# Both heads of an attention step in one instruction, projection groups in quarters on a bank of their own, bias tables asked for earlier, and x loaded tile by tile

## The reference, cut to what matters

```python
for l in range(DEPTH):                     # DEPTH = 4
    hp = modulate(rms_norm(xp, norm_g[l, 0]), sh1c, sc1c)
    if l % 2 == 0: yp = na_context(...); ys = na_latent(...)   # attention
    else:          yp = conv_module(...)                       # conv
    xp = xp + g1c * yp
    xp = xp + g2c * sq_relu_mlp(modulate(rms_norm(xp, ...)))
# attention, latent tokens: keys of an 8-row x 16-column neighbourhood
# with a relative bias, and 256 cached context keys without one
s_loc = einsum(q, k_block) * scale + bias;  s_ctx = einsum(q, k_ctx) * scale
p = softmax(concat([s_loc, s_ctx]));  o = p @ v
```

## Time and profile before

| | us |
|---|---|
| median of 3 runs | 2930.84 (2929.15 to 3099.0) |
| profiled execution, its own time | 2931.26 |
| its span, core 2, from first to last instruction | 2929.7 |
| spans of the eight cores | 2902.6 to 2929.7 |
| mean granted TensorE clock of core 2 | 0.930 |

### The profile page before, as it was taken

The page is one execution under the profiler, slowest core; times in us unless marked ns, Lnnn a source line. Parts: engine busy times, 40 slices in busy tenths (PEclk is TensorE's granted clock), DMA queues, the critical chain, the costliest instruction groups (busy, mean ns, idle before and its releaser), DMA issues.

```text
span 2929.7 us, 44923 instructions; the slowest of 8 cores (2902.6 to 2929.7 us)
## 1 busy us (share of the span) xinstructions
PE 2557.6 (87%) x15696; PEld 1130.2 (39%) x15696; DVE 1185.6 (40%) x1808; ACT 1068.7 (36%) x1887; POOL 208.6 (7%) x275
## 2 busy tenths in 40 slices
PE   1778778999998977999998788899999898789997
PEld 0323223444443532444443232234444354334443
DVE  0445444532324655423334444453232355642333
ACT  2435445520314345302233544563022424541123
POOL 1001010000000021000000010000000001200000
PEclk9879787999999988999999888899999998999998
DMA  9542233254542311444446222114553231113232
GB/s 196 115 80 37 41 55 66 43 102 89 110 90 44 66 28 33 77 96 94 94 73 124 41 41 41 34 30 87 97 105 72 44 75 33 30 29 58 44 58 87
DMA packets 107594, 202.24 MB, mean 69 GB/s; under 512 B 41904, under 2 KB 52144, under 8 KB 107376
## 3 DMA queue, kind: packets, MB, share of 16 engines
q0 software_dynamic: 76592, 154.23, 31.4%
q1 hardware_dynamic: 30784, 45.14, 4.7%
HBM read 315.02 MB, written 31.46 MB: 118 GB/s over the span
## 4 chain that ended last, share of the span: by engine, by line
PE 76%; DMA 7%; ACT 6%; issue 5%; DVE 5%; DVEq 0%; SPq 0%; ACTq 0%; POOL 0%; POOLq 0%
PE ps L639 44%; PE ps L1270 6%; PE ps L868 6%; DMA scr<-rpbp 3%; PE ps L661 3%; PE ps L825 3%; PE ps L1236 2%; PE ps L918 2%; PE ps L1394 2%; PE ps L963 2%; ACT hTs L617 2%; PE ps L567 1%; PE ps L921 1%; DMA xTs<-xT 1%; PE ps L977 1%
## 5 line engine op out<-in xcount | busy, mean ns | idle before, releaser
L639 PE MATMUL ps<-hTs,ring 128*128 128x512 bf16 x3072 | 687.5, 386 | 42.8 <-ACT hTs L617 41.8
L639 PE MATMUL ps<-big,ring 128*128 128x512 bf16 x3072 | 680.1, 379 | 0.4
L703 ACT ACTIVATE big<-ps 128x512 f32<-128x512 f32 x384 | 229.2, 597 | 801.1 <-PE ps L639 796.1
L639 PEld LDWEIGHTS ps<-hTs,ring 128*128 128x128 bf16 x3072 | 302.3, 99 | 416.1 <-issue 70.7
L705 DVE TENSOR_TENSOR big<-big 128x512 bf16<-128x512 f32 x384 | 266.0, 693 | 448.2 <-ACT big L703 448.2
L639 PEld LDWEIGHTS ps<-big,ring 128*128 128x128 bf16 x3072 | 299.4, 98 | 359.2
L677 DVE SCALAR_TENSOR_TENSOR xTs<-ps,mod,xTs 128x512 f32<-128x512 f32 x240 | 180.1, 751 | 551.1 <-PE ps L639 509.8
L560 ACT ACTIVATE scr<-xTs 128x512 bf16<-128x512 f32 x216 | 133.4, 626 | 409.4 <-DVE xTs L677 306.8
L936 ACT ACTIVATE scr<-scr 128x512 bf16<-128x512 f32 (+7 forms) x384 | 174.3, 500 | 258.8 <-DVE scr L988 125.5
L401 POOL DMA_DIRECT2D ring<-wall x140 | 100.1, 715 | 1896.9 <-PE ps L639 1003.8
L868 PE MATMUL ps<-hTs,ring 128*128 128x512 bf16 x768 | 226.2, 450 | 6.3 <-DVE scr L804 3.4
(11 more groups left out here) (90 smaller groups left out, 1916.5 us busy)
## 6 DMA issues: line engine op xcount, KB each, us to landing
ring<-wall POOLq DMA_DIRECT2D x140, 1024.0 KB, 9.8
vo<-big SPq DMA_DIRECT2D x48, 256.0 KB, 4.5
kTo<-big SPq DMA_DIRECT2D x48, 256.0 KB, 2.0
scr<-big SPq DMA_DIRECT2D x128, 54.0 KB, 3.1
xTs<-xT SPq DMA_DIRECT2D x3, 2048.0 KB, 25.3
yT<-scr SPq DMA_DIRECT2D x24, 256.0 KB, 2.2
scr<-rpbp POOLq DMA_DIRECT2D x32, 136.0 KB, 11.4
big<-ckT POOLq DMA_DIRECT2D x2, 512.0 KB, 7.3
```

Source lines behind the costliest of these rows:

```text
L639: ins = e.matmul(ps[pi][:, :], lhsT=w[:, kc, fc * fw:(fc + 1) * fw], rhs=src[:, kc, t * 512:(t + 1) * 512], start=(kc == 0), stop=(kc == n ...
L703: P.op("act", lambda e: e.activation(out=ta[:, :], in_=ps[pi][:, :], func=AF.Relu), reads=[ps_r[pi]], writes=[ta_r])
```

## The change

Five things change.

1. **Two heads, one instruction.** Banks 0 to 3 become two pairs of adjacent banks (`ps2`); step n uses pair n mod 2. The bias add and the exponential each treat both heads in one instruction of 128 x 2 x n. The add, exponential and table buffers are twice as long and half as many (2, 4, 2).
2. **Order and banks of the finish.** There are two output banks (5, 6) and one denominator bank (7). When the last step of a stretch has been multiplied, Ln is emitted, then the exponential of the step at hand, then Exp and the DVE multiply. The reciprocal lives in the conv taps' buffer `wr`, so the taps are now loaded at the start of each attention layer's MLP.
3. **Fills.** Projection groups are emitted as four parts of two matmuls, `build_T` stands behind each of the first four groups, and all of them, as well as the condition piece, use bank 4 (28 fills over 20 steps).
4. **Tables.** `hankel_load` for the pair after next stands at the end of a pair, ahead of `done_piece` and the condition piece; for pair 1 it stands before the first pair.
5. **x.** `xT` is stored tile by tile, in DRAM too, so that a tile is 16 KB in a row per partition, moved in rows of 8 KB in place of 2 KB. Tile 1 waits for weight piece 2 and tile 2 for piece 3. `norm_whole(1)` moves behind `ensure_h(0)` in front of value block 0, `norm_whole(2)` behind `ensure_h(1)` in front of block 4.

```diff
-    ps = [nc.alloc_psum_tensor(f"ps{i}", [128, 512], F32) for i in range(8)]
+    ps2 = [nc.alloc_psum_tensor(f"pp{i}", [128, 2, 512], F32) for i in range(2)]
+    ps = [ps2[i // 2][:, i % 2, :] for i in range(4)]
+    ps += [nc.alloc_psum_tensor(f"ps{i}", [128, 512], F32) for i in range(4, 8)]
...
-            out=xT[:, :, t * 512:(t + 1) * 512],
-            in_=xT_d.rearrange("(c p) t -> p c t", p=128)[:, :, t * 512:(t + 1) * 512]),
+            out=xT[:, t, :, :].rearrange("p c w -> p (c w)"), in_=xT_d[t], max_dma_last_dim=8192),
...
-            extra=[[], [(ring_sem[1], 16)], [(ring_sem[1], 32)]][t])
+            extra=[[], [(ring_sem[2], 16)], [(ring_sem[0], 32)]][t])
...
-        pi = next_ps(0, 4) if st.get("in_attn") else next_ps()
+        pi = 4 if st.get("in_attn") else next_ps()
...
+        if l % 2 == 0:
+            load_wr(l // 2)
...
-        NZ, NPT = 4, 8
+        NZ, NPT = 2, 4
+        rcp = wr[:, 0:1024].bitcast(F32)
...
-            pi = next_ps(0, 4)
+            pi = 4
...
-                if l == 0 and j == 0 and b == 4:
-                    late_x()
+                if l == 0 and j == 0 and b in (0, 4):
+                    ensure_h(b // 4)
+                    norm_whole(b // 4 + 1)
...
-            pi = next_ps(0, 4)
+            pi = next_ps() if pro else 4
...
+            if pro:
+                part(0, 8)
+                return []
+            return [lambda k0=k0: part(k0, k0 + 2) for k0 in range(0, 8, 2)]
...
-        OA = [4, 5]
-        SA = [6, 7]
+        hankel_load(2)
+        hankel_load(3)
+
+        OA, SA = [5, 6], 7
...
-                P.op("dve", lambda e: e.tensor_tensor(
-                    out=z[:, 0:n], in0=ps[b.pi][:, 0:n],
-                    in1=Tt[:, o0:o0 + k, :].rearrange("p o q -> p (o q)"), op=ALU.add),
-                    reads=[ps_r[b.pi], Tt_r], writes=[b.z_r])
+                P.op("dve", lambda e: e.tensor_tensor(
+                    out=z[:, :, 0:n], in0=ps2[pp][:, :, 0:n], in1=Tt[:, :, o0 * 64:o0 * 64 + n],
+                    op=ALU.add),
+                    reads=[ps_r[2 * pp], ps_r[2 * pp + 1], Tt_r], writes=[z_r])
...
+            P.op("act", lambda e: e.activation(out=pt[:, :, 0:n], in_=src[:, :, 0:n], func=AF.Exp),
+                 reads=src_r, writes=[pt_r])
...
+        def settle(n):
+            out = []
+            while len(pending) > n:
+                b, hp, o_i, last = pending.pop(0)
+                pv(b, hp, o_i)
+                if last is not None:
+                    finish_ln()
+                    out.append(lambda o_i=o_i, hp=hp, last=last: finish_mul(o_i, hp, last))
+            return out
...
-                hankel_load(2 * hp + 2)
-                hankel_load(2 * hp + 3)
...
+                for n in range(6):
+                    fills += qk_group(hp + 1, g[n][1], g[n][0], False)
+                    if n < 4:
+                        fills.append(lambda h=tb[n][0], hf=tb[n][1]: build_T(h, hf))
...
+                    pp = nstep % 2
+                    nstep += 1
                     q += 1
+                    scores(b, pp)
+                    if b.add is not None:
+                        b.add(pp)
                     while fills and (nf - len(fills) + 0.5) * nst <= q * nf:
                         fills.pop(0)()
-                    settle(LAG)
+                    pending.append((b, hp, o_i, tq if m == len(lst) - 1 else None))
+                    late = settle(LAG)
+                    exps(b, pp)
+                    for fn in late:
+                        fn()
...
+            if hp < 6:
+                hankel_load(2 * hp + 4)
+                hankel_load(2 * hp + 5)
             if hp % 2 == 0 and hp < 7:
                 done_piece()
...
-        if i == 0:
-            load_wr(1)
...
-    norm_whole(1)
```

More of the change, by code:

```diff
@@ new lines, in attn_layer, with ctx_step @@
+        class Step:
+            pass
+        def ctx_step(hp, qh, lc):
+            b = Step()
+            b.n, b.c0, b.first, b.v_r, b.add = 512, 0, lc == 0, cvb_r, None
+            b.ones = ones_c[:, :]
+            b.reads = [ckT_r, q_r[hp % 2][qh]]
+            b.lhs = lambda pb: ckT[pb:pb + 64, hp, lc * 128:(lc + 1) * 128]
+            b.rhs = lambda pb: qb[hp % 2][pb:pb + 64, qh * 512:(qh + 1) * 512]
+            b.gate = None
+            b.v = lambda h: cvb[:, lc, h * 64:(h + 1) * 64]
+            return b
@@ L959, in own_block, with own_step @@
+        def own_step(hp, qh, c, rows):
+            b = Step()
+            Tt, Tt_r = Tb[hp % 2]
             r0, k = rows[0], len(rows)
             n = k * 64
-            c0 = (r0 - qh * 8) * 64
+            b.n, b.c0, b.first, b.v_r = n, (r0 - qh * 8) * 64, False, V_r[c]
+            b.ones = ones_b[:, 0:64]
             b.reads = [k_r[hp % 2][c // 4], q_r[hp % 2][qh], gt_r]
-            b.mm_s = lambda e: e.matmul(
-                ps[b.pi][:, 0:n], lhsT=kb[hp % 2][pb:pb + 64, c * 128:(c + 1) * 128],
-                rhs=qb[hp % 2][pb:pb + 64, r0 * 64:r0 * 64 + n], start=True, stop=False,
-                skip_group_check=True)
+            b.lhs = lambda pb: kb[hp % 2][pb:pb + 64, c * 128:(c + 1) * 128]
+            b.rhs = lambda pb: qb[hp % 2][pb:pb + 64, r0 * 64:r0 * 64 + n]
+            b.v = lambda h: Vb[:, c, h * 64:(h + 1) * 64]
@@ L972, in own_block @@
             gidx = [k_ for k_, x_ in enumerate(gneed) if x_]
-            b.mm_g = None
+            b.gate = None
             if gidx:
@@ L1004, in slotb_block @@
             vb_i = k0 // 128
+            b.n, b.c0, b.first, b.v_r, b.add = 256, sq * 256, kc == 0, V_r[vb_i], None
+            b.ones = ones_b[:, 0:64]
             b.reads = [k_r[hp % 2][2], q_r[hp % 2][2]]
-            b.mm_s = lambda e: e.matmul(
-                ps[b.pi][:, 0:256], lhsT=kb[hp % 2][pb:pb + 64, k0:k0 + 128],
-                rhs=qb[hp % 2][pb:pb + 64, q0:q0 + 256], start=True, stop=True)
-            b.mm_g = None
-            b.add = None
-            b.exp = lambda: exp_to(b, ps[b.pi], ps_r[b.pi], 256)
@@ L1020, in fn, with scores @@
+            return b
+        def scores(b, pp):
+            n = b.n
             def fn(e):
                 ins = None
[L1022 to L1034 removed]
@@ L1035, in emit_scores @@
-            for b in blks:
-                b.exp()
+                for par in range(2):
+                    ins = e.matmul(ps[2 * pp + par][:, 0:n], lhsT=b.lhs(64 * par), rhs=b.rhs(64 * par),
+                                   start=True, stop=b.gate is None, skip_group_check=True)
+                if b.gate is not None:
+                    gs, gc, g0, g1 = b.gate
+                    for par in range(2):
+                        pb = 64 * par
+                        ins = e.matmul(ps[2 * pp + par][:, gs], lhsT=gt[pb:pb + 16, gc:gc + 128],
+                                       rhs=gt[pb:pb + 16, g0:g1], start=False, stop=True,
+                                       skip_group_check=True)
@@ new lines, in pv, with fn, fn2 @@
+        def pv(b, hp, o_i):
+            def fn(e):
+                ins = None
+                for par in range(2):
+                    ins = e.matmul(ps[o_i][64 * par:64 * par + 64, b.c0:b.c0 + b.n], lhsT=b.v(2 * hp + par),
+                                   rhs=b.pt[:, par, 0:b.n], start=b.first, stop=True,
+                                   skip_group_check=True)
+                return ins
+            P.op("pe", fn, reads=[b.v_r, b.pt_r], writes=[ps_r[o_i]])
+            def fn2(e):
+                ins = None
+                for par in range(2):
+                    ins = e.matmul(ps[SA][64 * par:64 * par + 64, b.c0:b.c0 + b.n], lhsT=b.ones,
+                                   rhs=b.pt[:, par, 0:b.n], start=b.first, stop=True,
+                                   skip_group_check=True)
+                return ins
+            P.op("pe", fn2, reads=[const_r, b.pt_r], writes=[ps_r[SA]])
@@ L1056, in attn_layer @@
+        npair, nstep = 0, 0
         st["in_attn"] = True
@@ L1063, in attn_layer @@
                     if rows:
-                        own.append(lambda par, qh=qh, c=c, rows=rows: own_block(hp, qh, par, c, rows))
-                ctx = [lambda par, qh=qh, lc=lc: ctx_block(hp, qh, par, lc) for lc in range(2)]
+                        own.append(own_step(hp, qh, c, rows))
+                ctx = [ctx_step(hp, qh, lc) for lc in range(2)]
                 steps.append((qh, ctx[:1] + own[:3] + ctx[1:] + own[3:]))
-            steps.append((2, [lambda par, sq=sq, kc=kc: slotb_block(hp, par, sq, kc)
-                              for sq in range(2) for kc in range(2)]))
+            steps.append((2, [sb_step(hp, sq, kc) for sq in range(2) for kc in range(2)]))
             nst = sum(len(x[1]) for x in steps)
@@ L1101, in attn_layer @@
                 adaln_piece()
-        settle(0)
+        for fn in settle(0):
+            fn()
         if ada_q:
```

202 lines of the change are left out of this document (64 added, 138 removed).

## The result

The change left the time within 2% of where it was, 0.8% longer: 2952.06 us, median of 5 runs (2947.39 to 3284.35), beside 2929.15 for five runs of the kernel before; the ratio is 1.0084 with a 95% interval from 1.0058 to 1.011. The profiled execution took 2947.39 us, 16 more than the one before (2931.26). Rows of after are those of core 2, the core of the rows before (its span: 2944.8 us against 2929.7), where nothing else is said. Some executions are longer by several per cent at a lower granted clock, most of them on the chips of the second and third set of experiments; ratios leave them out, so that intervals there are wide or missing.

The account below looks back on a forecast made before the run. Attention was taken as bound by TensorE together with waits in its strictly ordered list. 2931 us less both loops (664), less 17.5, plus 4, is 2253.5; loops back make 2312 + 14 T, so pairs of T = 46.5 give 2963, range 2865 to 3040.

Parts of the forecast that it names:

- the likeliest case: Whole kernel: a pair of 43 to 48.5 us, a time of 2914 to 2991 us; chance 0.55.
- its signs: Changed profile: projection start 53 to 66 us, table waits within 3, bank-4 waits 4 to 9 a pair, loops 340 to 370.
- Tables: Attention loops: requests ahead of weight loads remove nearly all of 37.4 and 20.4 us of TensorE waits.
- Two heads: Attention pairs: merged adds and exponentials give 0; ends -3.2 and +0.6 us a pair.
- Banks and order: Pairs with fills: waits on bank 4 and changeovers sum to 7.5 us a pair, taken as plus 6.1.
- Step 4: In a pair, table part and quarter back to back on bank 4: a wait of 4.4 us, plus 1.9.
- The size of a pair: Attention loops: 46.5 us for a pair with fills, between 36 and 53; the last pair 29.3.
- Bank 4 before the loop: First four table parts on one bank: three waits, 3.1 us; 2 us a layer taken, 4 in all, between 0 and 6.
- Start: Value projection begins at 57.8 us in place of 73.8, -16; tile 1's earlier norm makes it -17.5.
- half clock: Slower rival in the attention loops: waits pull the clock down, a pair of 53 us, 3054 us; chance 0.20.
- even flow: Faster rival in the loops: quarters fill TensorE's gaps, pairs of 40.4 or 36 us give 2878 or 2816; chance 0.20.
- Late tables: Rival: tables 3 us later than TensorE's other waits in 12 pairs, 36 us, giving 2999; chance 0.05.

Follow-up runs that it names:

- whole groups: Kernel after with each group of eight matmuls kept whole, ten fillings, one at every other step, on bank 4: 2873.68 us, 0.9677 of the kernel before.
- the spaced timetable: Kernel after with its 28 fills by another timetable: table parts in steps of their own, first table part and last quarter moved earlier: 0.9626 of the kernel before.
- the start alone: Kernel before with only the new layout of x, its loads tile by tile and the norms moved: 0.9936 of the kernel before.

## Why the prediction held, point by point

The forecast was 2963 us for a time within 2%; 2952 came, in the likeliest case. Of its signs, the start of value projection and the waits on bank 4 came as stated; the waits for tables, and in layer 2 the length of the loop (336.8 us, under the 340) and the clock (0.87, over the 0.85), missed their bars by a little. Of the 32 us that were forecast half came. That the total is off by no more is partly luck: the largest error, 18.0 us in layer 2, is offset by one of 5.5 the other way.

- **Tables.** The mechanism is shown both ways, in the trace and by putting the requests back. "At most 1 us is left each time" was a little too good: 8 waits with 17 us in all are left (the two rows above), the longest 3.5 us, against a bar of 3.
- **Two heads.** Taken as 0, measured as 0 (1.0081 beside 1.0084). The forecast of 1.21 and 1.1 us for the merged instructions met 1.22 and 1.06.
- **Banks and order.** This is where the gain went, at the steps named. The bar was 4 to 9 us a pair for the table add and the copies. The rows of L805, L890 and L882 shown above are 59.0 us in layer 0, 8.4 a pair, and 48.7 in layer 2, 7.0 a pair. Step 4 was priced too high: 4.4 us forecast, 2.6 on average in layer 0 (1.3 to 3.7). In the pair shown, idle time rose by 5.1 us and busy time fell by 0.7. The 0.1 us for each changeover was too much, as the text allowed: with the busy time that the traces show at a lower clock taken at full clock, seven pairs of layer 0 are 210 us of work in the kernel after, 203 before and 201 with whole groups, so 1.0 to 1.3 us a pair or some 0.06 for each of 18.
- **The size of a pair.** 46.5 us was taken. Layer 0 has 45.9 on average (41.9 to 50.9) and layer 2 43.7 (39.7 to 46.3). The step that was off is the one T for both layers. Layer 0 alone has the condition piece, whose wait on bank 4 (L478, 8.4 us) the list of stalls did not name. Layer 0's loop came within 2.2 us of the 354.8 forecast, layer 2's is 18.0 shorter. The last pairs, 31.7 and 30.9 us, did not fall to 29.3.
- **Bank 4 before the loop** was the other mis-sized term: 9.5 us, not 4, outside its 0 to 6. The three waits were priced well (3.9 us in the rows above, 3.1 forecast), but the deduction of 1 us a layer for what passes today was not, and that 16 matmuls behind the waits run at a clock of 0.55, 2.75 us, was not thought of.
- **Start.** -20.2 us against -17.5. Projection begins at 55.8, between the 57.8 taken and the 53 that the bytes alone would give; the wide rows landed in 18.9 us by the profile's page (median of the three tiles), 25.3 before, and the second tile, asked for 7.9 us later, landed 10.7 us earlier (32.78 + 17.95 against 24.86 + 36.58). The Trainium skill, "DMA: Bandwidth & Descriptors", section "Queues, rings and completion order", says that a DMA engine serves its queues in turn, a packet at a time, and by it the prediction put the gain near -21; -20.2 agrees. How much of it is the longer rows and how much the later request, no run here parts.
- **The clock.** 0.83 and 0.87 in the loops, where 0.82 and 0.85 stood before: the change did not pull it down, as the rival "half clock" had it, with a pair of 53 us. What the clock was worth only the spaced timetable showed.

The rival "even flow" was right about what the parts could do: it named 2816 us for a pair of 36, and with other spacing a pair is 36 and the time is 2827 at best. "Late tables" did not come: 17 us of waits for them are left in all. The change as made did not get there because of how its fillings hand the one bank over. The errors of the terms, summed: start -2.7, bank 4 before the loops +5.5, loops -2.2 and -18.0, against a forecast of +32 for the whole; what remains is +0.4 in stages not touched, and +15 came.

## What to carry to other kernels

When several producers share a PSUM bank, put the step that empties it into the timetable: let a filling come a step later than the one whose copy frees its bank, and put that copy ahead of a finish on the same engine. Here both together were worth some 130 us of 2952. Judge a short wait on TensorE by what it does to the granted clock too, and read both from the same stretch. Before merging instructions on an engine, look whether it ever holds up the bound one. And follow a gain ahead of a loop some steps into it before it is counted.

## What the runs showed that was not expected

- About half of what the spacing gained in layer 0, 34.6 of 68.4 us, was matmuls running at the higher clock (0.95 against 0.85). The Trainium skill, "TensorE: Matmul & The Clock Gate", section "A second HAM failure mode: psum-queue depth-cycling", describes a clock that swings when TensorE idles briefly between matmul groups that cycle through PSUM banks; the two kernels, which have the same instructions and differ in their short waits, agree.
- Ahead of the loop 5.0 us with 1.7 of TensorE work in them were followed by 6.20 us at a granted 0.55, for work that took 3.45 at 1.00 without the gaps.
- A mean clock can hide a level. In the whole groups' loop 0.87 came from 0.81 over 96 us, and not from more time at 0.50. That level does not hang on the program: with the start alone, cores 4 and 5 were granted it for over 430 us and cores 0 to 3 of the same execution not at all (spans of 2950 and 2954 us against 2892 to 2900).
